# The bias table goes out by pairs of heads in place of bands of rows

## The reference

```
dist = q_pos[:, None] - k_pos[None, :]
bias = jnp.transpose(rel_bias[t5_causal_bucket(dist)], (2, 0, 1)).astype(jnp.float32)
s = jnp.einsum('bhmqd,bhmkd->bhmqk', q_blk, kt).astype(jnp.float32) * scale + bias[None, :, None]
s = jnp.where(dist >= 0, s, -jnp.inf)
```

## Time and profile before

| | us |
|---|---|
| median of 3 runs | 2503.76 |
| lowest and highest | 2503.68, 2504.05 |
| profiled execution | 2503.76 |
| its span | 2502.0 |
| PE busy | 2475.8 (99%) |
| DVE busy | 1424.6 (57%) |
| ACT busy | 1220.3 (49%) |
| POOL busy | 26.1 (1%) |

### The profile page before, as it was taken

One profiled execution on the slowest core, in us unless ns is written; L12 is line 12 of the kernel. 1 busy time (PEld: TensorE's weight loads), 2 busy tenths in 40 slices (PEclk: granted clock), 3 DMA queues, 4 the chain that ended last, 5 costly groups with the idle time before them and its releaser, 6 DMA issues.

```text
span 2502.0 us, 32122 instructions
## 1 busy us (share of the span) xinstructions
PE 2475.8 (99%) x12059; PEld 2073.5 (83%) x12059; DVE 1424.6 (57%) x1926; ACT 1220.3 (49%) x1696; POOL 26.1 (1%) x46
## 2 busy tenths in 40 slices
PE   8999999999999999999999999999999999999998
PEld 6888887888888888888888898887888888888887
DVE  4568878676545455444446556667644545444444
ACT  5665457666444444444445555544544444444443
POOL 1000000000000000000000000000000000000000
PEclk9999999999999999999999999999999999999999
DMA  7765444555666666656666674333566666666664
GB/s 234 232 201 176 153 152 148 170 168 172 201 190 187 190 186 191 192 186 193 193 194 194 207 220 138 126 121 126 177 193 185 192 186 192 189 188 207 193 194 155
DMA packets 239013, 456.09 MB, mean 182 GB/s; under 512 B 16644, under 2 KB 25092, under 8 KB 238400
## 3 DMA queue, kind: packets, MB, share of 16 engines
q1 hardware_dynamic: 234896, 440.92, 58.2%
q0 software_dynamic: 4016, 13.79, 1.6%
HBM read 449.40 MB, written 5.24 MB: 182 GB/s over the span
## 4 chain that ended last, share of the span: by engine, by line
PE 96%; DVE 2%; ACT 1%; issue 0%; DMA 0%; POOL 0%; DVEq 0%; ACTq 0%; POOLq 0%
PE g L305 23%; PE g L307 23%; PE g L306 23%; PE g L1019 4%; PE g L1021 4%; PE g L1020 4%; PE g L1973 1%; PE g L1975 1%; PE g L1977 1%; PE m L1049 1%; PE m L655 1%; PE m L753 1%; DVE wl L293 1%; PE m L2056 0%; PE m L2080 0%
## 5 line engine op out<-in xcount | busy, mean ns | idle before, releaser
L293 DVE TENSOR_TENSOR wl<-raw,wh 128x1024 fp32r<-128x1024 f32 (+1 forms) x836 | 1015.6, 1220 | 931.2 <-ACT wh L289 928.2
L289 ACT ACTIVATE wh<-raw 128x1024 fp32r<-128x1024 f32 (+1 forms) x836 | 879.4, 1056 | 1094.9 <-PE g L307 918.8
L305 PE MATMUL g<-wh,act_hi 128*128 128x512 f32 x1800 | 705.5, 392 | 0.4 <-issue 0.4
L307 PE MATMUL g<-wh,act_lo 128*128 128x512 f32 x1800 | 701.1, 390 | 0.0
L306 PE MATMUL g<-wl,act_hi 128*128 128x512 f32 x1800 | 700.6, 389 | 0.0
L307 PEld LDWEIGHTS g<-wh,act_lo 128*128 128x128 f32 x1800 | 337.9, 188 | 70.9
L305 PEld LDWEIGHTS g<-wh,act_hi 128*128 128x128 f32 x1800 | 338.0, 188 | 70.2 <-issue 1.8
L306 PEld LDWEIGHTS g<-wl,act_hi 128*128 128x128 f32 x1800 | 338.1, 188 | 68.5
L305 PE MATMUL g<-wh,ht_hi 128*128 128x512 f32 x672 | 261.6, 389 | 0.0
L307 PE MATMUL g<-wh,ht_lo 128*128 128x512 f32 x672 | 261.4, 389 | 0.0
L306 PE MATMUL g<-wl,ht_hi 128*128 128x512 f32 x672 | 261.4, 389 | 0.0
(11 more groups left out here) (381 smaller groups left out, 2324.4 us busy)
## 6 DMA issues: line engine op xcount, KB each, us to landing
raw<-in_w_ffn_in SPq DMA_DIRECT2D x176, 512.0 KB, 3.6
raw<-in_ffn_w_in SPq DMA_DIRECT2D x176, 512.0 KB, 3.7
raw<-in_w_in SPq DMA_DIRECT2D x112, 512.0 KB, 4.4
raw<-in_w_ffn_out SPq DMA_DIRECT2D x88, 512.0 KB, 4.5
raw<-in_ffn_w_out SPq DMA_DIRECT2D x88, 512.0 KB, 4.2
raw<-in_nsa_w_in SPq DMA_DIRECT2D x80, 512.0 KB, 4.4
raw<-in_w_out SPq DMA_DIRECT2D x32, 512.0 KB, 4.5
raw<-in_nsa_w_out SPq DMA_DIRECT2D x32, 512.0 KB, 4.6
```

What stands on the lines that cost most here:

```text
L289: nc.scalar.activation(wh[:, j % SLOTS, 0:n], raw[:, j % SLOTS, 0:n], ACT.Copy).then_inc(hi_done, 1)
L293: nc.vector.tensor_tensor(wl[:, j % SLOTS, 0:n], raw[:, j % SLOTS, 0:n], wh[:, j % SLOTS, 0:n].bitcast(F32), ALU.subtract).then_inc(lo_don ...
L305: nc.tensor.matmul(dst, h, whk, start=(first and k == 0), stop=False)
L307: ins = nc.tensor.matmul(dst, l, whk, start=False, stop=(last and k == 1))
```

## The change

Before, a part is a band of 16 rows of all 24 heads, and there are 8 parts, each four units after the last. Now a part is all 128 rows of two heads, and there are 12 parts, each three units after the last. The first part still waits for unit 22 of `in1q`; the last waited for the unit 28 after that and now waits for the unit 33 after that.

```diff
-        BIAS_PARTS = 8
-        BIAS_ROWS = P // BIAS_PARTS
+        BIAS_PARTS = 12
...
             for n in range(BIAS_PARTS):
-                pool.wait_ge(lo_done, SLOTS + in1q_0 + 22 + 4 * n)
-                rows, r0 = bt[:, :], n * BIAS_ROWS
-                skewed = bass.AP(tensor=rows.tensor, offset=rows.offset + P - 1 - r0, ap=[list(rows.ap[0]), [-1, BIAS_ROWS], [1, S]])
-                pool.dma_start(dram_bias[:, r0:r0 + BIAS_ROWS, :], skewed).then_inc(bt_stored, 16)
+                pool.wait_ge(lo_done, SLOTS + in1q_0 + 22 + 3 * n)
+                rows = bt[2 * n:2 * n + 2, :]
+                skewed = bass.AP(tensor=rows.tensor, offset=rows.offset + P - 1, ap=[list(rows.ap[0]), [-1, P], [1, S]])
+                pool.dma_start(dram_bias[2 * n:2 * n + 2], skewed).then_inc(bt_stored, 16)
             pool.wait_ge(bt_stored, 16 * BIAS_PARTS)
```

## The result

The changed kernel is slower: 2527.61 us median of 4 runs (2526.11 to 2529.18) against 2503.72 us (2503.08 to 2504.05, 4 runs). The ratio is 1.0096, with a 95% interval of 1.0079 to 1.0113. The forecast of no change, given 0.88, was wrong; the 24 us are what rival B had priced (2518 to 2532 us) at 0.09.

A forecast was written before the change was run, and what follows sets the result against it. The prediction took TensorE, busy 2475.8 of 2502.0 us, to bound the kernel. Its four terms, each 0, were added to 2503.76 us to give 2503.8 us, with a range of 2502.8 to 2506.0 us.

The forecast's parts named there:

- rival B: Weight loads stand wholly behind a part on two engines, landing in 15.8 us: 2532 us, with half 2518; chance 0.09.
- TensorE had no wait to shorten: PE is busy for all 104 us from 114 to 218 us, so faster weight loads gain nothing.
- The bytes: Eight transfers of 384 KB become twelve of 256 KB, 3072 KB both times; only shape and moments move.
- the POOL issues: Four more issues on POOL at 0.69 us each, 2.8 us, with nobody waiting: priced 0.
- the cover of the later end: Parts done by 233 us at worst; first bias reader some 140 us later, ScalarE's wait 107 us later: priced 0.
- The landing of a part: A 256 KB part from two source rows lands in about 11 us, range 4.9 to 16.1.
- The slack of a weight load in plain units: In the first part of the stretch, a load may take 14.3 us before TensorE waits.
- The slack of the load ahead of the decays: In the recurrence, this load may take 8.4 us; each microsecond over is one of TensorE's, once a head.
- step 4: Parts' effect on weight loads, the only path to TensorE: loads of 5.4 to 7 us, under both limits, priced 0.
- the upper bound: Most that slower weight loads could cost: three heads, loads of 9.0 us against 8.4, 1.8 us.
- The second-block load: Load of sixteen heads, 2048 KB, 128 KB an engine; weight loads beside it took up to 9.0 us, PE stayed busy.
- The port rule of the Trainium skill: Neighbouring partitions share one port at 27.6 GB/s, so 256 KB take 9.5 us; parts longer by about the upper case.

The follow-up runs named there:

- f3_bands64: Changed kernel with two parts of 64 rows of all 24 heads, 1536 KB each, 18 units apart: 2502.73 us, ratio 1.0000.
- e2_one_head: Changed kernel with each two-head part issued as two one-head transfers at the same moment, 24 of 128 KB: 2530.47 us, ratio 1.0111.
- far pairs: Changed kernel with heads n and n + 12 in a part, source rows 12 partitions apart, same moments and bytes: 2503.14 us, ratio 1.0000.
- e1_bands12: Changed kernel with its twelve parts at the same moments, each a band of 10 or 11 rows of all 24 heads: 2503.97 us, ratio 1.0001.
- near pairs: Parts that read two neighbouring source partitions (heads 2n and 2n + 1), as the changed kernel itself does: 2527.61 us, ratio 1.0096.
- near halves: Changed kernel with a part every five units, each cut into two halves of 64 rows, one every two and a half units: 2503.62 us, ratio 0.9999.
- f1_step2: Changed kernel with the two source partitions of a part two apart, moments and bytes unchanged: 2535.75 us, ratio 1.0131.
- f2_step4: Changed kernel with the two source partitions of a part four apart: 2502.86 us, ratio 0.9998.
- e4_every5: Changed kernel with its parts every five units in place of three: 2523.35 us, ratio 1.0079.
- e7_four_near: Changed kernel with six parts of four neighbouring heads, 512 KB each, one every six units: 2577.73 us, ratio 1.0297.

## Why the prediction was wrong

**Right.** That TensorE had no wait to shorten, so nothing could be gained. The bytes, the POOL issues (1.06 us each in place of 0.69, still hidden) and the cover of the later end: the load that waits for all parts went out at 261.37 us in place of about 233 (the parts are issued by units, and the units ran late), and nobody waited for it. The landing of a part: 15.8 us median, inside the range of 4.9 to 16.1, at its upper end and not near the 11 us that I took, with 19.6 us at most above it. The slack of a weight load in plain units, 14.3 us: f3_bands64 had one of 12.8 and lost nothing, and the one of 14.7 in the changed kernel cost TensorE half a microsecond. The slack of the load ahead of the decays, 8.4 us: in f3_bands64 it took 8.0 and PE waited for nothing.

**The step that failed** is step 4, at "how long will loads take": "If each packet of a load waits for one of a part, its 32 KB on an engine take 1.5 us more: about 5.4 us, at most 7". Two things were wrong in it. The pace of a part's packets came from a stretch in which sixteen engines read memory and wrote all 128 partitions, 22.1 GB/s each; two engines that read neighbouring partitions share some 22 GB/s, 12 for each busy engine, so each packet holds its engine about twice as long, and longer still when two parts overlap (0.04 MB in 2 us on 3.3 engines, 6 GB/s each, from 127 to 129 us). And strict turns were too kind: in 4 us of e2_one_head no packet of weights came between 44 of the parts. Loads then landed in 11.8 us median and 19.4 at most, over the limits of 8.4 and 14.3 us.

The same mistake made the upper bound too low. The second-block load moves 128 KB on each engine, which I called the nearest row for a heavier load, and beside it loads took 9.0 us. It matches in bytes per engine, but it spreads them over all partitions. In the far pairs, with as many bytes on two engines, loads took 10.4 us at most and PE lost nothing; so bytes per engine alone would indeed have been hidden.

**Rival B** had the place and the price. Its 11.9 us, worked out from even sharing of an engine, met the measured 11.6 us by luck: what sets it is the source, since the far pairs took 10.7 - 4.2 = 6.5 us for the same bytes on as many rows. The 4.2 us in both sums is itself too high, as the 3.7 us of e1_bands12 shows; the gap of 5.1 us between near and far pairs does not depend on it. B's shares were off too: it put 22 us on the decays of the recurrence and 6 on plain units, and the trace has 12.9 us at the decays and 9.6 at units that wait for `wl`. Its "wholly behind a part" is nearly what the runs show, but not quite: in f3_bands64 the load issued at about 115.0 us landed at 127.8, ahead of the band issued at 113.4, which took at least 15.6. How an engine divides itself between the two queues is open; no view shown here separates the packets of one engine.

What the runs do show is a threshold. Near pairs (15.8 us to landing) cost 1.6 to 2.0 us each, alone or not; near halves (8.5 us to landing) and far pairs (10.7) cost nothing; parts of four neighbours (26.8) cost 74.4 / 6 = 12.4 us each. That is what a slack that must be used up first would do. The length of a part alone does not set it: the two bands of 64 rows landed in 15.9 us, as late as a near pair, and cost nothing. Beside them the loads took 12.8 us at most, where near pairs made them take up to 19.4. The chain that gave way most was the one named as tightest, the decays of the recurrence (12.9 of 23.0 us). Its limit of 8.4 us holds only for the one load in eight that it was read from, as the harmless load of 11.3 us just ahead of it in f3_bands64 shows. The longest load beside the far pairs, 10.4 us, says nothing of this limit: it was issued at 114.7 us among plain units.

The port rule of the Trainium skill (SBUF — State Buffer, "Door 1: The DMA port swizzle") was cited in the prediction and set aside: it "says nothing of loads queued behind them". The traces agree roughly with its 27.6 GB/s for one port (22 to 29 GB/s here) and, as far as f1_step2 and f2_step4 test them, with its groups of four. What I left out was the step from a slow source to the other transfers on the same engines. By that step the rule was a case of rival B, and should have had most of its chance.

**What the clock added** was in no term: 9 to 10 us of 32 in the profiled execution came from the lower granted clock after the waits.

## What to carry to other kernels

A transfer that is itself in nobody's way can still be slow for its own reasons, and every engine that carries it is then slow for all others; so ask of a reshaped transfer not only when it lands but at what pace its packets leave the source, and bound that by a row with the same source, not the same bytes. Spread the source rows of a side transfer over partitions at least four apart, or keep each transfer short. Compare how long the transfers that matter may take, at their tightest chain, with how long they take beside it. That comparison held here: loads of 12.8 us against a limit of 14.3 and of 8.0 against 8.4 cost nothing, and one of 14.7 us against 14.3 cost half a microsecond.

## What the runs showed of the hardware

- Four neighbouring partitions give some 22 to 29 GB/s to transfers together, whether a transfer reads one of them (e2_one_head), two (e4_every5) or four (e7_four_near), and whether some two, four or sixteen engines are busy with it.
- A transfer from such a source makes other transfers late: weight loads of 4.6 us median took 11.8 beside near pairs, and 5.3 beside far pairs of the same bytes.
- Sixteen engines can be busy at a share of 1.03 and move 29 GB/s. The DMA share alone does not tell a full engine from a held one; the share with the GB/s does.
- Short transfers from the same partitions hold their engines less: 25 GB/s for each busy engine at 16 rows, 14 at 64 rows. Why is open.
- No version beat the kernel before: the eight runs that stayed beside it have ratios from 0.9998 to 1.0001, as is to be expected where TensorE had no wait in that stretch.
